# Adding up the squares of a normalisation on GpSimd, with one matmul with ones behind the first weight chunk

## The chip, the cores and the metric

The kernel runs on one core of one Trainium2 chip. The metric is the device time of the whole kernel in microseconds (us), here the median of 3 runs.

## The reference

A first block and a two-layer second block work on 256 tokens of width 1024 (the first one with 16 meta tokens ahead: 272). There are six normalisations in the change's sense, in this order: before the first block's mixer (norm 0), before its FFN (norm 1), the final one of the first block together with the one before the second block's even mixer (norm 2, two sums), before the first MLP (norm 3), before the odd mixer (norm 4) and before the last MLP (norm 5). Each of them is

```python
ms = jnp.mean(xf * xf, axis=-1, keepdims=True)
y  = xf * lax.rsqrt(ms + EPS) * g
```

and what follows is a matrix product of y with a weight matrix. The FFN is `(silu(u @ w_gate) * (u @ w_up)) @ w_down`, an MLP is `square(relu(h @ w1)) @ w2`.

## The kernel before

**Layout.** Everything is kept with the features on the 128 partitions and the tokens along the free dimension: `x_all` is 8 feature blocks of 272 tokens. The mean over the features is therefore a sum over partitions and over 8 blocks, and it is made on TensorE: a matmul of a 128x128 matrix of ones with the squares of one block, accumulated over 8 blocks, leaves the sum on every partition. The root of it is taken late: the projections work on `u = x * gain`, and what comes out of them is multiplied by `rms` (1/root) when it is read out of PSUM.

**Split matmuls.** Weights and activations are held as a high and a low part (`whi`, `wlo` and `u[:, 0]`, `u[:, 1]`), and a product is three matmuls. ScalarE makes the high part of a weight chunk (L967), VectorE the low part (L1317, recorded at L1304), and the same holds for `u`: ScalarE `u_hi`, VectorE the low half (`lo_pair`, L1348, recorded at L1307), pair of blocks by pair, which raises `u_ready`.

**Weight chunks.** SyncE streams chunks of at most 128x2048 through a ring of 4. A chunk of 256 output columns is two groups of 8 x 3 = 48 matmuls in all, into two of four PSUM banks (`proj`), by turns; `proj_free` says that VectorE has read them out.

**The normalisation.** ScalarE, in `norm` (L1083), makes for each of four pairs the two `u_hi` and the squares of the pair (`sq_ready`), in norm 2 also the squares for the second sum; then it waits for `sumsq`, takes the square root (`root`, L975, with a table load ahead of it) and raises `root_ready`. VectorE's `norm_scale` (L1598) makes the reciprocal and raises `rms_ready`. In norm 2 a second root and reciprocal follow (L1670 to L1677).

**The ones matmuls.** TensorE's first chunk behind a normalisation has a gate, `by_pair` (L404): ahead of blocks 0, 2, 4 and 6 of its first half it waits for `u_ready` of that pair. From norm 1 on the gate also issues the ones matmuls of the pair before it (`square_pair`, L437), and at block 6 those of the last pair as well:

```python
if k % 2 == 0:
    if norm_no and k:
        square_pair(k // 2 - 1, norm_no, **sums)
    if norm_no and k == 6:
        square_pair(3, norm_no, **sums)
    pe.wait_ge(sems["u_ready"], 4 * norm_no + k // 2 + 1)
```

So `sumsq` is raised in the middle of the chunk's first half. In norm 0 all eight stand behind the first chunk (L474). The first chunk is rq0 (norm 0), the first up chunk of the FFN (norm 1), sq0 (norm 2), the first up chunk of the first MLP (norm 3), the gates chunk with 8 columns (norm 4) and the first up chunk of the last MLP (norm 5).

**The hidden layers** (`hidden_layer`, L698 on TensorE, L1602 on VectorE): TensorE does up chunk 0, up chunk 1, then the down chunk of hidden block 0 into `aux`, and from then on up and down by turns in a loop. The down chunk waits for `hidden_ready`. VectorE's order ahead of it is: reciprocal of the norm, the low part of one more weight chunk, then the first hidden block (with ScalarE's tanh in the FFN and ScalarE's high part in both), then its low half.

**GpSimd** has two instructions in the whole kernel (L1291, L1293), for the first block's attention. Each instruction of VectorE, ScalarE and GpSimd here is followed by a wait for its own semaphore (`Lane.post`).

## Time and profile before

| | |
|---|---|
| median of 3 runs | 1213.16 us (1211.6 to 1213.25) |
| the profiled execution: its span | 1212.2 us |
| TensorE matmul busy | 1131.0 us, 93%, 8618 records |
| TensorE weight loads busy | 1072.7 us, 88% |
| VectorE busy | 786.8 us, 65%, 865 records |
| ScalarE busy | 514.3 us, 42%, 509 records |
| GpSimd busy | 6.0 us, 6 records |
| DMA | 175.70 MB, 145 GB/s in the mean |

The profile gives no time of its own for the profiled execution beside the span; the median of the timed runs is 0.9 us above the span. The span counts from the start of the first record to the end of the last. Busy time of TensorE is modelled (matmuls overlap with the next one), so the starts of matmuls are what is read for a rate. One matmul of 32-bit floats with `ones` leaves two records, one split matmul leaves one. DVE is VectorE, ACT is ScalarE, POOL is GpSimd, PE is TensorE. In brackets at a row's end stands how long the engine had been idle before it and who ended that.

### The profile page before, as it was taken

What the parts mean: (1) busy time and instruction counts of PE and PEld (TensorE: products, weight loads), DVE (VectorE), ACT (ScalarE), POOL (GpSimd) and SP (SyncE); (2) the same over time, 40 slices, a digit from 0 to 9 for tenths busy, and PEclk for the clock granted to TensorE, in tenths of its full rate; (3) what the DMA queues carried; (4) which work ended last, traced back from release to release, by engine and by line L of the source; (5) the groups of instructions that cost most, each with busy time, mean ns of one, the idle gap of its engine ahead of it and who ended that gap; (6) DMA issues with size and microseconds to landing.
All of it is one profiled execution on the core that took longest, in us unless ns stands there. A gap on an engine that the chain in (4) does not pass through costs nothing.

```text
span 1212.2 us, 20954 instructions
## 1 busy us (share of the span) xinstructions
PE 1131.0 (93%) x8618; PEld 1072.7 (88%) x8618; DVE 786.8 (65%) x865; ACT 514.3 (42%) x509; POOL 6.0 (0%) x6
## 2 busy tenths in 40 slices
PE   5998999799899999988986999999988999999998
PEld 4996777588899999988875999999988899999997
DVE  4765778577656665667677565555469787655553
ACT  5323443333444444446274543433244356434331
POOL 0000001000000000000000000000000000000000
PEclk9998999799999999999997999999988999999999
DMA  8743135034435656563421365564343434655630
GB/s 259 228 139 105 40 106 172 8 124 134 140 90 170 192 173 205 166 215 127 161 95 44 131 209 171 176 207 132 113 139 105 143 114 162 208 184 167 202 104 35
DMA packets 160534, 175.70 MB, mean 145 GB/s; under 512 B 4433, under 2 KB 146769, under 8 KB 160353
## 3 DMA queue, kind: packets, MB, share of 16 engines
q1 hardware_dynamic: 160480, 174.95, 45.7%
q8 instruction: 39, 0.64, 0.2%
q14 instruction: 15, 0.11, 0.0%
HBM read 173.89 MB, written 1.05 MB: 144 GB/s over the span
## 4 chain that ended last, share of the span: by engine, by line
PE 77%; DVE 15%; ACT 5%; issue 2%; DMA 0%; SPq 0%; DVEq 0%; ACTq 0%
PE proj L384 47%; PE aux L725 20%; DVE f L1307 4%; DVE wlo L1304 4%; DVE f L1304 2%; PE aux L441 2%; DVE f L1310 1%; ACT whi L967 1%; PE aux L652 1%; PE aux L528 1%; PE aux L635 1%; DVE x_all L1304 1%; DVE v L1307 1%; PE aux L522 1%; PE aux L645 0%
## 5 line engine op out<-in xcount | busy, mean ns | idle before, releaser
L384 PE MATMUL proj<-u,whi 128*128 128x256 f32 (+1 forms) x2912 | 540.7, 287 | 18.9 <-DVE wlo L1304 8.9
L384 PEld LDWEIGHTS proj<-u,whi 128*128 128x128 f32 x2912 | 457.5, 192 | 28.9 <-issue 19.9
L1304 DVE TENSOR_TENSOR wlo<-raw,whi 128x2048 fp32r<-128x2048 f32 (+2 forms) x175 | 374.1, 2137 | 145.0 <-ACT whi L967 138.4
L384 PE MATMUL proj<-u,wlo 128*128 128x256 f32 (+1 forms) x1456 | 414.5, 285 | 0.0
L967 ACT ACTIVATE whi<-raw 128x2048 fp32r<-128x2048 f32 (+2 forms) x175 | 313.5, 1791 | 131.3 <-PE proj L384 78.1
L384 PEld LDWEIGHTS proj<-u,wlo 128*128 128x128 f32 x1456 | 279.8, 192 | 0.0
L725 PE MATMUL aux<-v,whi 128*128 128x256 f32 x1376 | 249.9, 283 | 1.7 <-DVE v L1304 1.5
L725 PEld LDWEIGHTS aux<-v,whi 128*128 128x128 f32 x1376 | 214.2, 192 | 2.4 <-issue 2.4
L725 PE MATMUL aux<-v,wlo 128*128 128x256 f32 x688 | 194.6, 283 | 0.0
L725 PEld LDWEIGHTS aux<-v,wlo 128*128 128x128 f32 x688 | 131.9, 192 | 0.0
L384 PE MATMUL proj<-v,whi 128*128 128x256 f32 (+2 forms) x592 | 112.5, 292 | 9.2 <-DVE v L1304 3.7
L384 PEld LDWEIGHTS proj<-v,whi 128*128 128x128 f32 (+1 forms) x592 | 94.0, 194 | 13.3 <-issue 10.8
L1138 ACT ACTIVATE v<-f 128x512 fp32r<-128x512 f32 x32 | 20.2, 632 | 166.8 <-DVE f L1304 166.8
L384 PE MATMUL proj<-v,wlo 128*128 128x256 f32 (+2 forms) x296 | 84.9, 287 | 0.0
L384 PE MATMUL proj<-whi,u 128*128 128x256 f32 (+1 forms) x352 | 68.1, 289 | 5.5 <-DVE f L1310 2.5
L384 PEld LDWEIGHTS proj<-whi,u 128*128 128x128 f32 x352 | 57.6, 197 | 7.3 <-issue 5.6
L1304 DVE TENSOR_TENSOR v<-f,v 128x512 fp32r<-128x512 f32 (+2 forms) x56 | 34.0, 607 | 38.5 <-ACT v L1138 24.7
L384 PEld LDWEIGHTS proj<-v,wlo 128*128 128x128 f32 (+1 forms) x296 | 57.3, 193 | 0.0
L1304 DVE TENSOR_TENSOR f<-proj,r_all 128x512 f32<-128x512 f32 (+6 forms) x67 | 40.9, 610 | 22.2 <-PE proj L384 19.7
L1310 DVE TENSOR_SCALAR f<-proj 128x512 f32<-128x512 f32 x32 | 22.1, 692 | 44.6 <-PE proj L384 44.0
L384 PE MATMUL proj<-wlo,u 128*128 128x256 f32 (+1 forms) x176 | 50.2, 285 | 0.0
L1131 ACT ACTIVATE proj<-f 128x256 f32<-128x256 f32 x22 | 8.5, 388 | 66.0 <-DVE f L1304 66.0
(248 smaller groups left out, 842.4 us busy)
## 6 DMA issues: line engine op xcount, KB each, us to landing
raw<-in_mlp_w_dram SPq DMA_DIRECT2D x64, 1024.0 KB, 5.4
raw<-in_w_in_dram SPq DMA_DIRECT2D x22, 1024.0 KB, 5.3
raw<-in_od_w_in_dram SPq DMA_DIRECT2D x12, 1024.0 KB, 5.5
raw<-in_w_ffn_gate_dram SPq DMA_DIRECT2D x22, 512.0 KB, 4.0
raw<-in_w_ffn_up_dram SPq DMA_DIRECT2D x22, 512.0 KB, 5.3
raw<-in_w_ffn_down_dram SPq DMA_DIRECT2D x21, 512.0 KB, 5.5
raw<-in_ev_w_in_dram SPq DMA_DIRECT2D x10, 1024.0 KB, 5.9
raw<-in_w_ret_out_dram SPq DMA_DIRECT2D x4, 1024.0 KB, 5.4
```

The lines of the kernel that those rows point to most:

```text
L384: ins = mm(o, w_of(a, k), x_of(b, k), start=first and k == 0 and j == 0, stop=last and k == kt - 1 and j == 2, skip_group_check=skip)
L441: ins = mm(aux[:, 0, 0:tokens], C("ones"), sq_of(tokens)[:, k, :], start=k == 0, stop=k == KT - 1, skip_group_check=True)
L522: ins = mm(o, k_ret[p0:p0 + 64, h // 2, t:t + m], q_ret[p0:p0 + 64, h // 2, :], start=True, stop=True)
L528: ins = mm(aux[:, 2 * (h % 2) + 1, S:2 * S], rv_tok[0:m, j, h * P:(h + 1) * P], sd[0:m, h % 2, j, :], start=j == 0, stop=j == 2)
L635: ins = mm(aux[:, b, 0:L], q_all[0:96, h, b * P:(b + 1) * P], k_all[0:96, h, :], start=True, stop=True)
L652: ins = mm(aux[p0:p0 + 64, 3, S:2 * S], v_tok[0:m, j, 64 * h:64 * h + 64], pt[0:m, j, :], start=j == 0, stop=j == 2)
L725: ins = mm(aux[:, j // 2, (j % 2) * S:(j % 2 + 1) * S], W(a, n, 0, kt, D)[:, q, j * P:(j + 1) * P], v[:, b, 2 * (k % 2) + q, :], start=fir ...
L967: A.post(act(whi[:, n % RING, 0:wd], raw[:, n % RING, 0:wd], ACT.Copy), "hi_ready")
L1138: A.post(act(v[:, 0, 2 * (k % 2):2 * (k % 2) + 2, :], f("f1", 512, 2, S), ACT.Copy), "hidden_hi")
L1304: return ve.tensor_tensor(o, a, b, op)
L1307: return ve.scalar_tensor_tensor(out=o, in0=a, scalar=s, in1=b, op0=op0, op1=op1)
L1310: return ve.tensor_scalar(o, a, s, s2, op) if op2 is None else ve.tensor_scalar(o, a, s, s2, op, op2)
```

## The change

The squares are no longer summed over the blocks on TensorE. GpSimd gets a function `add_squares`: when the squares of pair c are ready it adds that pair to pair 0 (an operation of 128x512, in place; in norm 2 one for each sum), and after pair 3 it adds block 1 to block 0 (128x256) and raises `sq_added` (and `second_added`). TensorE's gate only waits for `u_ready`. Behind the whole first chunk `sum_squares` waits for `sq_added` and issues one ones matmul, in norm 2 two. Nothing else is changed. In norm 0 the operations are 128x544 and 128x272 wide.

```diff
--- before.py
+++ after.py
@@ -401,14 +401,10 @@
             def finish(ins):
                 ins.then_inc(sems["chunk_used"], 1)
 
-            def by_pair(norm_no, **sums):
+            def by_pair(norm_no):
 
                 def gate(k):
                     if k % 2 == 0:
-                        if norm_no and k:
-                            square_pair(k // 2 - 1, norm_no, **sums)
-                        if norm_no and k == 6:
-                            square_pair(3, norm_no, **sums)
                         pe.wait_ge(sems["u_ready"], 4 * norm_no + k // 2 + 1)
                 return gate
 
@@ -434,19 +430,14 @@
                                    lambda a, k: W(a, n, 0, KT, width)[:, k, :], KT, gate=gate if j == 0 else None)
                 finish(ins)
 
-            def square_pair(c, norm_no, tokens=S, second=False):
-
-                pe.wait_ge(sems["sq_ready"], 4 * norm_no + c + 1)
-                for k in (2 * c, 2 * c + 1):
-                    ins = mm(aux[:, 0, 0:tokens], C("ones"), sq_of(tokens)[:, k, :], start=k == 0, stop=k == KT - 1,
-                             skip_group_check=True)
-                if second and c:
-
-                    for k in range(0 if c == 1 else 2 * c, 2 * c + 2):
-                        ins = mm(aux[:, 1, 0:S], C("ones"), f("f3", 0, KT, S)[:, k, :], start=k == 0, stop=k == KT - 1,
-                                 skip_group_check=True)
-                if c == 3:
-                    ins.then_inc(sems["sumsq"], 1)
+            def sum_squares(norm_no, tokens=S, second=False):
+
+                pe.wait_ge(sems["sq_added"], norm_no + 1)
+                ins = mm(aux[:, 0, 0:tokens], C("ones"), sq_of(tokens)[:, 0, :], start=True, stop=True)
+                if second:
+                    pe.wait_ge(sems["second_added"], 1)
+                    ins = mm(aux[:, 1, 0:S], C("ones"), f("f3", 0, KT, S)[:, 0, :], start=True, stop=True)
+                ins.then_inc(sems["sumsq"], 1)
 
             def turn_norm(norm_no):
 
@@ -471,8 +462,7 @@
             project("rq0", t0=META, t=S, gate=by_pair(0))
             pe.wait_ge(sems["const_in"], 16)
             pe.wait_ge(sems["x_ready"], KT)
-            for c in range(4):
-                square_pair(c, 0, L)
+            sum_squares(0, L)
             project("rq1", t0=META, t=S)
             project("rk0")
             read_out("rq1")
@@ -733,6 +723,7 @@
 
                 pe.wait_ge(sems["proj_free"], order[g - 1] if order[g - 1] % 2 else order[g - 1] + 1)
                 up(g, 0, gate=by_pair(norm_no))
+                sum_squares(norm_no)
                 pe.wait_ge(sems["proj_free"], order[g - 1] + 1)
                 up(g + 1, 1)
                 pe.wait_ge(sems["rms_ready"], norm_no + 1)
@@ -748,7 +739,8 @@
 
 
             pe.wait_ge(sems["hidden_val"], M0["k0"])
-            project("sq0", t0=META, t=S, gate=by_pair(2, second=True))
+            project("sq0", t0=META, t=S, gate=by_pair(2))
+            sum_squares(2, second=True)
             for name in ("sq1", "sk0", "sk1"):
                 project(name, t0=META, t=S)
             turn_norm(2)
@@ -854,6 +846,7 @@
 
             pe.wait_ge(sems["hidden_val"], M1["k0"])
             project_tokens("gates", 8, gate=by_pair(4))
+            sum_squares(4)
             project("qk0", t0=META, t=S, between=lambda: turn_norm(4))
 
             pe.wait_ge(sems["gates_ready"], 1)
@@ -1286,11 +1279,26 @@
             G = Lane(eng, sems, "pool_step")
             gp = nc.gpsimd
 
+            def add_squares(norm_no, tokens=S, second=False):
+
+                pairs = [(sq if tokens == L else f("f2", 0, KT, S), "sq_added")]
+                if second:
+                    pairs.append((f("f3", 0, KT, S), "second_added"))
+                for c in range(1, 4):
+                    eng.wait_ge(sems["sq_ready"], 4 * norm_no + c + 1)
+                    for t, _ in pairs:
+                        G.run(gp.tensor_tensor(t[:, 0:2], t[:, 0:2], t[:, 2 * c:2 * c + 2], ALU.add))
+                for t, name in pairs:
+                    G.post(gp.tensor_tensor(t[:, 0], t[:, 0], t[:, 1], ALU.add), name)
+
+            add_squares(0, L)
             eng.wait_ge(sems["kr_roped"], 1)
             eng.wait_ge(sems["kv_half"], 1)
             G.post(gp.tensor_copy(k_all[64:96, :, :], bc(kr[64:96, :], 8)), "kr_copied")
             eng.wait_ge(sems["q_mla_rotated"], 2)
             G.post(gp.tensor_tensor(q_pre[0:96], q_pre[0:96], bc(C("cos_mla")[0:96, META:L], 8), ALU.mult), "q_cos")
+            for norm_no in range(1, 6):
+                add_squares(norm_no, second=norm_no == 2)
 
 
         @block.vector
```

TensorE's queue at the first up chunk of the FFN (norm 1) before, from the chunk's sixth split matmul on; L384 is a split matmul, L441 a ones matmul:

```order
L441 MATMUL aux<-f,cst 128x256 x2
L384 MATMUL proj<-u,whi 128x256 x2
L384 MATMUL proj<-u,wlo 128x256
L384 MATMUL proj<-u,whi 128x256 x2
L384 MATMUL proj<-u,wlo 128x256
L441 MATMUL aux<-f,cst 128x256 x2
L384 MATMUL proj<-u,whi 128x256 x2
L384 MATMUL proj<-u,wlo 128x256
L384 MATMUL proj<-u,whi 128x256 x2
L384 MATMUL proj<-u,wlo 128x256
L441 MATMUL aux<-f,cst 128x256 x4
```

and after the change, from the end of that chunk (L436 is the ones matmul, in front of it stand the 48 of the chunk):

```order
L384 MATMUL proj<-u,whi 128x256 x2
L384 MATMUL proj<-u,wlo 128x256
L436 MATMUL aux<-f,cst 128x256
L384 MATMUL proj<-u,whi 128x256 x2
L384 MATMUL proj<-u,wlo 128x256
L384 MATMUL proj<-u,whi 128x256 x2
```

The ones matmul that raises `sumsq` has moved from behind the chunk's 18th split matmul to behind its 48th, and the eight have become one.

GpSimd's queue before (the first three rows are the program's start):

```order
L2036 MEMSET const-bfloat16-1.0 128x1
L2036 MEMSET const-uint8-127 128x1
L1284 UNCONDITIONAL_BRANCH
L1291 COPY f<-kr 32x2176
L1293 ISA
L1293 TENSOR_TENSOR f<-f,cst 96x2048
```

and after the change, from norm 0 to norm 2:

```order
L1290 TENSOR_TENSOR f<-f 128x544 x3
L1292 TENSOR_TENSOR f<-f 128x272
L1297 COPY f<-kr 32x2176
L1299 TENSOR_TENSOR f<-f,cst 96x2048
L1290 TENSOR_TENSOR f<-f 128x512 x3
L1292 TENSOR_TENSOR f<-f 128x256
L1290 TENSOR_TENSOR f<-f 128x512 x6
L1292 TENSOR_TENSOR f<-f 128x256 x2
```

The two old instructions stand behind the adds of norm 0; each of the norms 3 to 5 adds three rows of 128x512 and one of 128x256 more.

## Rows read from the trace of the kernel before

**Rows 1.** Busy times by stretch (PE, PEld, DVE, ACT, POOL, PEclk, DMA): last MLP

```profile
1042.00:1190.00 148.00, 148.00 (x1244) 148.00 (x1244) 86.99 (x66) 56.27 (x39) 0.00 (x0) 1.00 0.49 163
```

**Rows 2.** The ones matmuls' line: min/median/max ns, first and last start

```profile
L441 PE MATMUL aux<-f,cst x96: 377/379/774, 27.8 to 1022.5; 128*128 128x256 f32 x80, 128*128 128x272 f32 x16
```

**Rows 3.** Timeline of GpSimd: start us, us, engine, line, operation, tiles, form

```profile
210.37 3.82 POOL L1293 TENSOR_TENSOR f<-f,cst 96x2048 f32<-96x2048 f32 x1 [1.03 <-PE aux L606]
```

**Rows 4.** Timeline at norm 1 (FFN), TensorE, VectorE and ScalarE, by start

```profile
343.63 0.50 PE L384 MATMUL proj<-u,whi 128*128 128x256 f32 x2 [0.85 <-DVE x_all L1304]
...
344.28 1.03 DVE L1307 SCALAR_TENSOR_TENSOR u<-x_all,par,u 128x256 fp32r<-128x256 f32 x2 [0.70 <-ACT u L1094]
...
344.75 0.63 ACT L1095 ACTIVATE f<-x_all 128x512 f32<-128x512 f32 x1
...
347.56 1.89 PE L441 MATMUL aux<-f,cst 128*128 128x256 f32 x8
...
349.53 1.28 ACT L976 ACT_TABLE_LOAD   x1 [4.15 <-PE aux L441]
...
353.35 2.29 DVE L1304 TENSOR_TENSOR wlo<-raw,whi 128x2048 fp32r<-128x2048 f32 x1 [0.19 <-ACT whi L967]
...
359.46 0.42 DVE L1304 TENSOR_TENSOR v<-f,v 128x256 fp32r<-128x256 f32 x1 [0.61 <-ACT v L1134]
...
360.04 0.47 PE L725 MATMUL aux<-v,whi 128*128 128x256 f32 x2 [1.37 <-DVE v L1304]
```

**Rows 5.** Timeline at norm 2 (two sums), by start

```profile
548.80 1.03 DVE L1307 SCALAR_TENSOR_TENSOR u<-x_all,small,u 128x256 fp32r<-128x256 f32 x2 [1.70 <-ACT u L1094]
...
549.93 1.05 ACT L1100 ACTIVATE f<-x_all,par 128x256 f32<-128x256 f32 x2
...
553.02 2.29 DVE L1304 TENSOR_TENSOR wlo<-raw,whi 128x2048 fp32r<-128x2048 f32 x1 [3.20 <-ACT whi L967]
...
553.81 1.28 ACT L976 ACT_TABLE_LOAD   x1 [0.89 <-PE aux L446]
...
566.65 0.50 PE L384 MATMUL proj<-u,whi 128*128 128x256 f32 x2 [3.73 <-DVE wlo L1304]
```

**Rows 6.** Timeline at norm 3 (first MLP)

```profile
691.34 1.28 ACT L976 ACT_TABLE_LOAD   x1 [4.16 <-PE aux L441]
```

**Rows 7.** Timeline at norm 4 (gates)

```profile
878.32 2.05 DVE L1307 SCALAR_TENSOR_TENSOR u<-x_all,par,u 128x256 fp32r<-128x256 f32 x4
...
885.29 0.47 ACT L976 ACTIVATE r_all<-aux,small 128x256 f32<-128x256 f32 x1 [3.25 <-PE aux L441]
...
887.81 4.62 DVE L1304 TENSOR_TENSOR wlo<-raw,whi 128x2048 fp32r<-128x2048 f32 x2 [0.19 <-ACT whi L967]
...
898.22 0.60 PE L862 MATMUL aux<-cst,small 128*4 128x128 f32 x4 [1.76 <-DVE small L1307]
```

**Rows 8.** Timeline at norm 5 (last MLP)

```profile
1017.14 0.40 PE L384 MATMUL proj<-u,whi 128*128 128x256 f32 x2
...
1019.33 1.03 DVE L1307 SCALAR_TENSOR_TENSOR u<-x_all,par,u 128x256 fp32r<-128x256 f32 x2 [0.70 <-ACT u L1094]
...
1022.96 1.28 ACT L976 ACT_TABLE_LOAD   x1 [2.53 <-PE aux L441]
```

**Rows 9.** Busy times by stretch (PEclk is the granted clock), norms 2 and 4

```profile
567.40:570.80 3.40, 3.40 (x18) 3.40 (x18) 3.37 (x2) 0.00 (x0) 0.00 (x0) 0.50 0.92 293
...
875.00:885.00 10.00, 10.00 (x33) 8.65 (x33) 7.35 (x11) 5.61 (x8) 0.00 (x0) 0.51 0.00 0
```

**Rows 10.** Timeline at norm 0, VectorE and TensorE

```profile
26.42 6.95 DVE L1304 TENSOR_TENSOR wlo<-raw,whi 128x2048 fp32r<-128x2048 f32 x3
...
33.62 1.85 DVE L1370 RECIPROCAL r_all<-r_all 128x272 f32<-128x272 f32 x1 [0.25 <-ACT r_all L976]
...
35.51 0.69 DVE L1304 TENSOR_TENSOR f<-proj,r_all 128x512 f32<-128x512 f32 x1
...
37.16 0.42 PE L384 MATMUL proj<-u,whi 128*128 128x272 f32 x2
```

## The prediction

> **What bounds the kernel now.** I read the page first: TensorE is busy for 93% of the span, so a change that takes matmuls away looks like a gain of their length. I then read the timeline of every place where the removed matmuls stand, because an average says nothing about what a place is worth. There are six: the normalisations 0 to 5, each in the first weight chunk behind it.
>
> In the long hidden loops TensorE is the bound: 148.0 of 148.0 us busy with 1,244 matmuls at the full clock [rows 1], so one split matmul of 256 columns takes 0.119 us, and a chunk of 48 takes 5.7 us. A ones matmul has two records: [rows 2] counts 96 at L441, which are 48 matmuls, and 8 more stand in the second sum of norm 2. The group of four in [rows 4] takes 1.89 us with the tail of its last one, so one costs about 0.43 us. The change keeps 7 of 56, and 49 x 0.43 = **21.1 us** of TensorE's work go. That is the number one would like to forecast, and I don't.
>
> The reader is to see in [rows 4] what waits for these matmuls. In the FFN the last four start at 347.56, ScalarE begins the table load for the root at 349.53, VectorE makes the reciprocal, splits a weight chunk (353.35, 2.29 us), then comes the first hidden block, and its low half is written from 359.46 for 0.42 us. TensorE meanwhile does the rest of chunk one and all of chunk two, is out of work, and starts the down projection at 360.04 **after waiting 1.37 us for that low half**. The chain from the root's start to the down projection is 360.04 - 349.53 = 10.5 us, and nothing in the change shortens it. What counts in this place is therefore when the sum leaves TensorE, not how much TensorE works.
>
> **The change, place by place.** The last ones matmul moves from the middle of the first chunk to behind it. From the start of the last one to the root's start is 349.53 - (347.56 + 3 x 0.43) = 0.7 us, and stays so.
>
> *Norm 1 (FFN).* TensorE starts the chunk at 343.63; u is complete when VectorE's two operations from 344.28 end, 345.31, before the fourth pair is due (343.63 + 18 x 0.119 = 345.8). So the chunk runs through: 343.63 + 5.7 = 349.3, one ones matmul from there to 349.8, the root at 350.0. That is **0.5 us later than 349.53**, although seven matmuls fewer were done. GpSimd has to be ready by 349.3: the last squares end at 344.75 + 0.63 = 345.4, then one add of 512 and one of 256. The nearest row is its product of 96x2048 in 3.82 us [rows 3]: by its elements 0.95 and 0.48 us, at worst 3.82 each. I take the first, since the row is the same operation, and GpSimd is ready at 347. The chain then puts the down projection at 360.04 + 0.5. TensorE ends chunk two at 349.8 + 5.7 = 355.5 and now waits 5.0 us where it waited 1.4. Net: **+0.5 us**.
>
> *Norm 3 (first MLP).* The same shape, with the root's start at 691.34 [rows 6]. The down projection starts there without a listed wait, so its chain and chunk two end together; now the one comes 0.5 us later and the other 3 us earlier: some 3.5 us of waiting. **+0.5 us**.
>
> *Norm 5 (last MLP).* Here u is complete late: 1019.33 + 1.03 = 1020.4, when TensorE, started at 1017.14, has long done its 18 matmuls. It waits, then does 30 more (3.6 us) to 1024.0, root at 1024.7 against 1022.96 [rows 8]. **+1.7 us**, and again some 4 us of waiting before the down projection.
>
> *Norm 2 (two sums).* Sixteen ones matmuls fill the time between pairs of u; the root starts at 553.81 [rows 5]. Without them TensorE waits for each pair: ScalarE has five operations per pair and VectorE ends the last low half at 548.80 + 1.03 = 549.8. The last squares end at 549.93 + 1.05 = 551.0. GpSimd then has two adds of 512 and two of 256, 2.9 us by the low price: 553.9. TensorE's last 30 matmuls end at 553.4 at the full clock and, if part of them runs at half clock, at 555 to 556. With two ones matmuls the root starts between 555.0 and 558. I take 557, **+3.2 us**. Behind it stands a chain of root, two reciprocals, a second root and the first lo split of chunk sk0, for which TensorE already waits 3.73 us (566.65), so all of it counts.
>
> *Norm 4 (gates).* The chunk's columns are 8 wide and TensorE stood at half clock there: 0.51 from 875 to 885 [rows 9]. Now it waits for u_ready until 880.4, then issues 30 of these at 0.21 us (half clock): 886.7, and the root at 887.9 with the ones matmul at half clock, against 885.29. VectorE's two splits behind the reciprocal end at 887.81 + 4.62 = 892.4 now, about 1 us before TensorE's turned factors come; they will end 2.6 us later, so the transposes at 898.22 start about **1.7 us** later [rows 7]. At the full clock the same sum gives -1.6 us, the other end.
>
> *Norm 0.* Seven of eight ones matmuls go, 3.0 us, and chunk rq1 starts earlier, though not before its lo half, the first of three splits from 26.42 on, at 28.7. Chunk rk0 needs rq0's bank, and VectorE frees it only behind all three splits (33.37), a reciprocal of 1.85 us and 0.69 us for the bank [rows 10]: 36.0 where TensorE started at 37.16. **-1.1 us**.
>
> The sum is 0.5 + 0.5 + 1.7 + 3.2 + 1.7 - 1.1 = **+6.5 us**.
>
> **What the new waits do to the clock.** The granted clock was 0.50 from 567.4 to 570.8, right behind the wait of 3.73 us that ended at 566.65, and 18 matmuls ran there where 0.119 us each would have made 28 [rows 5, 9]. The new waits before the down projections of norms 1, 3 and 5 are 5.0, 3.5 and about 4 us, and behind each TensorE is the bound. I take one such stretch and a little more each, 1.9 us; the ends are nothing and 3.4 us. **+5.7 us**. The Trainium skill (TensorE: Matmul & The Clock Gate, Part 1) says that the default state is the slow one and that activity releases it; that rule speaks against a change that takes filler work off TensorE where it waits, and by it the sum is +12.2, without it +6.5.
>
> Together **+12.2 us**. Sum and rows are of one execution with a span of 1212.2 us; the median of the timed runs is 0.9 us above that span, and I add the difference to the median: 1213.2 + 12.2 = 1225.4 us.
>
> **The rivals.** (a) *The clock stays up* at the three down projections: 1213.2 + 6.5, about **1220 us**; with norms 2 and 4 at their low ends (+1.2 and -1.6) it is +1.2 in all, 1214. For it: the wait of 1.37 us in [rows 4] is short, and the waits of 3.5 and 4 us may be shorter than I make them. Against it: the one wait as long as these in the rows was followed by it.
>
> (b) *GpSimd and VectorE get in each other's way, or an add costs far more than 0.95 us.* The adds of norm 2 would meet the split at 553.02 (2.29 us), and those of norm 5 the low halves of u; one operation of VectorE in front of the last add and one add in front of u's low half cost 2.3 + 1.0 us in norm 2 and 1.0 in norm 5. That is 4 us more, about **1230 us**. With adds of 3.8 us norms 1, 3 and 5 have 7.6 us of adds where 3.9 us are free (345.4 to 349.3), 3.7 us more each, **1238 us** or beyond. No row here shows the two engines reading SBUF at once with two SBUF inputs on VectorE's side. The Trainium skill (SBUF — State Buffer, section SBUF: two separate sides) has the port pair that the two share as an exclusive lock, held for a whole instruction, for a VectorE operation with two SBUF inputs; no run here shows that so far.
>
> (c) *The other side, faster:* TensorE's busy time is what bounds, and the chain from the sum to the first hidden block fits behind chunk two. The point from which it decides is a chain of no more than the 5.7 us of that chunk. Then each removed matmul counts: 1213.2 - 21.1 = **1192 us**. For it: the 93%. Against it: the chain measures 10.5 us, and TensorE waits for it already, with 3 us more of cover. For a small gain it would be enough that norms 2 and 4 gain instead of losing.
>
> (d) *No change:* the later roots cost less than worked out (the chain has slack that [rows 4] doesn't show, at norms 3 and 5), and the -1.1 of norm 0 and a gain in norm 4 balance the rest: **1213 us**.
>
> **How the numbers follow.** Forecast, chains and clock: 0.52. (a) 0.20, (b) 0.15, (d) 0.08, (c) 0.05. The range has to hold 8 in 10. Its low end takes in (a), 1216, its high end the 1230 of (b) and clock stretches of twice the length, 1233; the 1238 of (b), (c) and (d) stay outside. A measurement of this kernel can tell about 0.2%, 2.4 us, from no change. Slower by over that: forecast, (b), nearly all of (a), 0.86; within it: (d) and the low end of (a), 0.09; faster: 0.05.
>
> **What would show it.** In the changed profile TensorE's busy time should fall by less than 21 us as modelled ends stretch at half clock, its waits in the first chunks of norms 2, 4 and 5, and before the down projection's first matmul, should rise from 1.4 to about 5 us (FFN) and from nothing to some 3.5 to 4 us (both MLPs), with the table load of the root 0.5 us later counted from the chunk's start. The clock should be at half behind them. The release of the root by GpSimd instead of by the chunk's end would show (b); no wait before the down projections would show the forecast wrong, and a span under 1200 us would mean that I misread what bounds these places.

## The result, and the profile after

The changed kernel takes **1237.4 us** (median of 5 runs, 1234.55 to 1239.85), the kernel before, timed beside it, 1213.05. The ratio is 1.0207, interval 1.0194 to 1.022: **24.3 us slower**, where the forecast had 12.2. The direction was right, and the time lies outside the range of 1216 to 1233.

Part 1 of the page after, TensorE's busy time first:

```profile
span 1235.4 us, 20803 instructions
## 1 busy us (share of the span) xinstructions
PE 1126.9 (91%) x8520; PEld 1070.9 (87%) x8520; DVE 800.2 (65%) x865; ACT 514.2 (42%) x509; POOL 43.9 (4%) x34
```

98 matmul records are gone (49 matmuls of two records each), and TensorE's busy time fell by 4.1 us, not by 21: matmuls that run at the half clock are counted longer. I added up the stretches in which the granted clock is at its lower level, 1.2 GHz: 81.1 us before, 138.1 after. The rise is largest in the even mixer (17.1 to 37.5 us), in norm 2 up to its root (4.7 to 15.5) and in the odd mixer (13.7 to 21.0).

The two traces can be cut at the same instructions: the first matmul of the chunk behind each norm, the activation of its root (1.3 us behind the table load's start), and the first down matmul. What each step takes more than before:

| step | forecast | measured |
|---|---|---|
| norm 0 and the first mixer | -1.1 | -3.94 (see the last experiment) |
| norm 1: chunk to root; root to down | +0.5; 0 | +0.53; 0.00 |
| FFN's loop behind its first down | +1.9 | +2.48 |
| norm 2: chunk to root | +3.2 | **+5.36** |
| even mixer: that root to norm 3's chunk | 0 | **+4.97** |
| norm 3: chunk to root; root to down | +0.5; 0 | +0.55; 0.00 |
| first MLP's loop | +1.9 | +1.44 |
| norm 4: chunk to root | part of the next | **+4.36** |
| odd mixer, up to norm 5's chunk | +1.7 with norm 4 | -0.19 |
| norm 5: chunk to root; root to down | +1.7; 0 | **+5.09**; 0.00 |
| last MLP's loop | +1.9 | +2.51 |
| sum | +12.2 | +23.2 |

The sum is that of two single executions, 1.1 us under the difference of the medians.

**The FFN and the MLPs went as forecast.** Timeline after at norm 1, TensorE, ScalarE and GpSimd; it answers to [rows 4]:

```profile
341.58 1.29 POOL L1290 TENSOR_TENSOR f<-f 128x512 f32<-128x512 f32 x1 [3.71 <-ACT f L1088]
342.95 0.73 POOL L1292 TENSOR_TENSOR f<-f 128x256 f32<-128x256 f32 x1
346.12 1.28 ACT L969 ACT_TABLE_LOAD   x1 [4.67 <-PE aux L436]
356.62 0.77 PE L715 MATMUL aux<-v,whi 128*128 128x256 f32 x2 [4.95 <-DVE v L1312]
...
710.51 0.77 PE L715 MATMUL aux<-v,whi 128*128 128x256 f32 x2 [3.67 <-DVE v L1312]
...
1052.84 0.77 PE L715 MATMUL aux<-v,whi 128*128 128x256 f32 x2 [3.64 <-DVE v L1312]
```

GpSimd is done at 343.7, long before the chunk's end. The waits are 4.95, 3.67 and 3.64 us where 5.0, 3.5 and about 4 were worked out. The clock behind them (windows: PE busy and count, PEld, DVE, ACT, POOL, PEclk, DMA share, GB/s; the second window is in the last MLP):

```profile
355.40:362.20 6.80, 5.58 (x26) 5.61 (x27) 3.38 (x7) 3.29 (x5) 0.00 (x0) 0.50 0.60 162
1052.80:1058.50 5.70, 5.66 (x26) 5.69 (x27) 3.68 (x3) 1.80 (x2) 0.00 (x0) 0.50 0.48 144
1057.00:1185.00 128.00, 128.00 (x1071) 128.00 (x1070) 74.86 (x58) 50.98 (x35) 0.00 (x0) 0.99 0.57 189
```

In 5.7 us 26 matmuls run where 48 would at the full clock. Afterwards the loop runs as in [rows 1], and what it lost is never won back.

**Norm 2 did not.** VectorE, GpSimd, ScalarE and TensorE after, answering to [rows 5]:

```profile
544.53 8.71 POOL L1290 TENSOR_TENSOR f<-f 128x512 f32<-128x512 f32 x6 [200.85 <-ACT f L1093]
545.15 5.61 DVE L1315 SCALAR_TENSOR_TENSOR u<-x_all,small,u 128x256 fp32r<-128x256 f32 x4
550.81 0.79 PE L384 MATMUL proj<-u,whi 128*128 128x256 f32 x2 [1.18 <-DVE u L1315]
552.09 3.31 DVE L1312 TENSOR_TENSOR wlo<-raw,whi 128x2048 fp32r<-128x2048 f32 x1 [1.33 <-ACT whi L960]
553.33 3.47 POOL L1292 TENSOR_TENSOR f<-f 128x256 f32<-128x256 f32 x2
557.56 0.59 PE L439 MATMUL aux<-f,cst 128*128 128x256 f32 x2
558.23 1.28 ACT L969 ACT_TABLE_LOAD   x1 [6.25 <-PE aux L439]
571.06 0.79 PE L384 MATMUL proj<-u,whi 128*128 128x256 f32 x2 [7.24 <-DVE wlo L1312]
```

The split at 552.09 takes 3.31 us, not the 2.29 of [rows 5]. The arithmetic of these rows is that of whole instructions taking turns. The six adds end at 544.53 + 8.71 = 553.24. The split waits for that, 1.15 us at most, and is 1.02 us longer. GpSimd's next add starts at 553.33, the split ends at 555.40: 2.07 us of waiting and two adds of 0.73 make 3.5, and the row has 3.47. GpSimd ends at 553.33 + 3.47 = 556.80. TensorE starts the 30 matmuls behind the last pair at 550.81 and the first ones matmul at 557.13, so they took 6.3 us where 3.6 would do at the full clock; the granted clock was at half there until 556.8. The two chains end within 0.4 us of each other, and both are late: making only one of them faster gains little. In the kernel with fillers below, TensorE is done first and waits for GpSimd, and norm 2 is still 4.78 us longer than before:

```profile
554.34 0.70 PE L443 MATMUL aux<-f,cst 128*128 128x256 f32 x2 [1.47 <-POOL f L1300]
```

Behind the root the wait for sk0's low half grew from 3.73 to 7.24 us, and the clock is at half behind that, too:

```profile
567.40:577.60 10.20, 6.54 (x31) 6.54 (x32) 9.88 (x10) 2.89 (x3) 0.00 (x0) 0.52 0.55 182
604.60:611.40 6.80, 6.80 (x28) 5.87 (x27) 4.37 (x3) 0.00 (x0) 0.00 (x0) 0.50 0.12 43
```

The second window lies 45 us behind the root. TensorE is full there in both kernels; the window at the same distance in the trace of before has 59 matmuls:

```profile
600.20:607.00 6.80, 6.80 (x59) 6.63 (x61) 4.44 (x4) 0.00 (x0) 0.00 (x0) 1.00 0.29 88
```

Followed matmul by matmul, the even mixer loses 1.2 us directly behind the wait, 3.1 us in the stretch 45 us behind the root and some 0.6 us in waits near its end. The long wait is no sufficient reason for the second stretch. With the adds alone (first experiment) the wait is longer still and the stretch is missing; in the hybrid (below) the wait is that of before and the stretch is there. Each pair is the matmul behind the wait and the window 44 to 52 us behind the root, adds alone first:

```profile
568.59 0.80 PE L384 MATMUL proj<-u,whi 128*128 128x256 f32 x2 [8.52 <-DVE wlo L1324]
602.00:608.80 6.80, 6.80 (x55) 6.27 (x53) 4.17 (x3) 0.00 (x0) 0.00 (x0) 1.00 0.24 74
```

```profile
560.12 0.51 PE L384 MATMUL proj<-u,whi 128*128 128x256 f32 x2 [3.68 <-DVE wlo L1320]
592.30:599.10 6.80, 6.80 (x27) 5.83 (x26) 4.46 (x3) 0.00 (x0) 0.00 (x0) 0.50 0.13 45
```

**Norm 4**, after, VectorE, GpSimd and TensorE, answering to [rows 7]:

```profile
886.93 1.37 POOL L1290 TENSOR_TENSOR f<-f 128x512 f32<-128x512 f32 x1 [188.11 <-ACT f L1088]
887.22 1.89 DVE L1315 SCALAR_TENSOR_TENSOR u<-x_all,par,u 128x256 fp32r<-128x256 f32 x2
889.13 1.27 POOL L1290 TENSOR_TENSOR f<-f 128x512 f32<-128x512 f32 x1 [0.82 <-ACT f L1088]
889.14 0.69 DVE L1315 SCALAR_TENSOR_TENSOR f<-aux,r_all 128x512 f32<-128x512 f32 x1
889.87 1.08 DVE L1312 TENSOR_TENSOR x_all<-x_all,f 128x512 f32<-128x512 f32 x1
892.04 0.37 PE L384 MATMUL proj<-whi,u 128*128 128x8 f32 x1 [1.44 <-DVE u L1315]
899.74 1.20 PE L436 MATMUL aux<-f,cst 128*128 128x256 f32 x2
912.87 1.01 PE L855 MATMUL aux<-cst,small 128*4 128x128 f32 x4 [3.71 <-DVE small L1315]
```

While GpSimd adds (889.13 to 890.40), an operation that reads PSUM (`aux`) takes its usual 0.69 us, and the one behind it, with both inputs in SBUF, 1.08 instead of 0.69. From the last wait to the ones matmul TensorE issues 36 narrow matmuls in 7.7 us. I had counted 30 from the fourth pair on; at half clock TensorE was still busy with the third pair when the fourth came. The transposes behind the turned factors wait 3.71 us where [rows 7] had 1.76, and lie 3.3 us later, counted from the chunk's start, where 1.7 was forecast. The root is 4.36 us later there, so 1.1 us is won back between the root and the transposes.

**Norm 5**, after, answering to [rows 8]:

```profile
1027.94 1.53 POOL L1290 TENSOR_TENSOR f<-f 128x512 f32<-128x512 f32 x1 [132.98 <-ACT f L1088]
1028.35 1.93 DVE L1315 SCALAR_TENSOR_TENSOR u<-x_all,par,u 128x256 fp32r<-128x256 f32 x2
1032.96 1.51 POOL L1290 TENSOR_TENSOR f<-f 128x512 f32<-128x512 f32 x1 [3.48 <-ACT f L1088]
1033.36 1.91 DVE L1315 SCALAR_TENSOR_TENSOR u<-x_all,par,u 128x256 fp32r<-128x256 f32 x2
1037.77 0.56 PE L384 MATMUL proj<-u,whi 128*128 128x256 f32 x2 [1.48 <-DVE u L1315]
```

Two of u's low halves are longer by 0.9 us each, and both stand on the way to the last pair. TensorE then runs at half clock inside the chunk; the 30 matmuls from 1037.77 to the ones matmul at 1042.94 take 5.2 us where 3.6 would do:

```profile
1038.10:1041.50 3.40, 3.40 (x18) 3.40 (x17) 0.00 (x0) 0.00 (x0) 1.83 (x2) 0.50 0.00 0
```

### The profile page after: what moved, and what is told of

It reads as the page before. It is cut to its first block, busy times and chain, and to the rows that moved or that the text cites. A ratio compares the mean times of both kernels' runs of the same rounds, so it can differ in the third digit from the quotient of the medians.

```text
span 1235.4 us, 20803 instructions
## 1 busy us (share of the span) xinstructions
PE 1126.9 (91%) x8520; PEld 1070.9 (87%) x8520; DVE 800.2 (65%) x865; ACT 514.2 (42%) x509; POOL 43.9 (4%) x34
## 4 chain that ended last, share of the span: by engine, by line
PE 71%; DVE 19%; ACT 7%; issue 3%; DMA 0%; SPq 0%; DVEq 0%; ACTq 0%
PE proj L384 44%; PE aux L715 20%; DVE wlo L1312 5%; DVE f L1315 4%; DVE f L1312 3%; DVE u L1315 2%; ACT whi L960 2%; DVE f L1318 1%; PE aux L642 1%; DVE x_all L1312 1%; PE aux L625 1%; DVE v L1315 1%; PE aux L635 0%; DMA f<-in_x_dram 0%; PE aux L518 0%
## 5 line engine op out<-in xcount | busy, mean ns | idle before, releaser
L384 PE MATMUL proj<-u,whi 128*128 128x256 f32 (+1 forms) x2912 | 547.1, 289 | 33.0 <-DVE u L1315 12.6
L384 PEld LDWEIGHTS proj<-u,whi 128*128 128x128 f32 x2912 | 463.0, 194 | 44.3 <-issue 21.7
L384 PE MATMUL proj<-u,wlo 128*128 128x256 f32 (+1 forms) x1456 | 417.6, 287 | 0.0
L384 PEld LDWEIGHTS proj<-u,wlo 128*128 128x128 f32 x1456 | 283.4, 195 | 0.0
L715 PE MATMUL aux<-v,whi 128*128 128x256 f32 x1376 | 255.9, 287 | 12.4 <-DVE v L1312 12.4
L715 PEld LDWEIGHTS aux<-v,whi 128*128 128x128 f32 x1376 | 219.3, 196 | 13.1 <-issue 13.1
L715 PEld LDWEIGHTS aux<-v,wlo 128*128 128x128 f32 x688 | 134.9, 196 | 0.0
L384 PE MATMUL proj<-v,whi 128*128 128x256 f32 (+2 forms) x592 | 112.6, 292 | 9.2 <-DVE v L1312 3.7
L384 PEld LDWEIGHTS proj<-v,whi 128*128 128x128 f32 (+1 forms) x592 | 94.0, 194 | 13.3 <-issue 10.8
L384 PE MATMUL proj<-v,wlo 128*128 128x256 f32 (+2 forms) x296 | 85.1, 287 | 0.0
L384 PE MATMUL proj<-whi,u 128*128 128x256 f32 (+1 forms) x352 | 72.3, 300 | 11.0 <-DVE u L1315 5.9
L384 PEld LDWEIGHTS proj<-whi,u 128*128 128x128 f32 x352 | 61.9, 212 | 13.0 <-issue 6.0
L1290 POOL TENSOR_TENSOR f<-f 128x512 f32<-128x512 f32 (+1 forms) x21 | 30.8, 1465 | 816.3 <-ACT f L1088 596.6
L384 PEld LDWEIGHTS proj<-v,wlo 128*128 128x128 f32 (+1 forms) x296 | 57.4, 194 | 0.0
L384 PE MATMUL proj<-wlo,u 128*128 128x256 f32 (+1 forms) x176 | 52.4, 298 | 0.0
```

What stands on the lines that cost most here:

```text
L384: ins = mm(o, w_of(a, k), x_of(b, k), start=first and k == 0 and j == 0, stop=last and k == kt - 1 and j == 2, skip_group_check=skip)
L715: ins = mm(aux[:, j // 2, (j % 2) * S:(j % 2 + 1) * S], W(a, n, 0, kt, D)[:, q, j * P:(j + 1) * P], v[:, b, 2 * (k % 2) + q, :], start=fir ...
L1290: G.run(gp.tensor_tensor(t[:, 0:2], t[:, 0:2], t[:, 2 * c:2 * c + 2], ALU.add))
```

## The experiments

Three theories. **A**: GpSimd's adds hold up VectorE, by rival (b)'s lock. **B**: the sum comes later, because it stands behind 48 matmuls and not inside the chunk. **C**: what is lost is the clock, since matmuls that filled TensorE's waits are gone. Each ratio is against the kernel before, run beside it; where two of the kernels are compared, it is by their medians. The kernel before had medians between 1212.2 and 1213.3 beside the different experiments, so such a comparison can be off by about 1 us.

**Adds alone.** The kernel before, with GpSimd's adds into an unused tile, and ScalarE waiting for them ahead of the root:

```diff
+                eng.wait_ge(sems["sq_added"], norm_no + 1)
                 eng.wait_ge(sems["sumsq"], norm_no + 1)
...
+            for norm_no in range(1, 6):
+                add_squares(norm_no, second=norm_no == 2)
```

> The kernel before, its 56 ones matmuls all in place, with GpSimd's adds made as in the change but into a scratch region that only the root waits for (the result isn't used). Theory A (GpSimd's adds and VectorE's operations with two SBUF inputs hold each other up): the low halves of u stretch as in the changed kernel, 5.4 us for four in norm 0 and 5.6 us for four in norm 2, and of the 24 us some 5 to 8 are here, 1218 to 1221 us, from norms 2, 4 and 5. Theory B (only the later sum costs) and theory C (only the clock, by the missing matmuls): GpSimd works beside and the time is that of before, 1213 within 1.5 us.

Measured: 1223.44, ratio 1.0086 (1.0069 to 1.0103), **+10.4** by the ratio. Norm 2's root is 4.44 later, norm 5's 1.58, norm 4's 0.66; norms 1 and 3 0.04. There, too, low halves of u meet an add and take 0.9 us longer (1.92 us for two, 1.01 before), but VectorE would have waited for TensorE behind them. Adds whose result nobody uses cost 6.7 us in the norms, within the 5 to 8 expected. A holds. The total is above the 1218 to 1221 of the expectation: the even mixer takes 1.59 and the odd one 2.62 us more, and the first one 2.5 us less in this one trace. The kernel of memsets below has such losses in the mixers without an add, so they can't be put down to A.

**Move alone.** No GpSimd; all 8 (16) ones matmuls behind the chunk.

```diff
                 up(g, 0, gate=by_pair(norm_no))
+                for c in range(4):
+                    square_pair(c, norm_no)
```

> The kernel before without GpSimd, with its eight (in norm 2 sixteen) ones matmuls all behind the first chunk. Theory B: the root starts later by about 3.4 us in norms 1 and 3 than before (chunk 5.7 us and then eight matmuls of 0.43 us), 3.5 or more in norm 5, 3 to 6 in norm 2 and 2 to 3 in norm 4, and all of it counts: 1228 to 1232 us. If only GpSimd matters (theory A alone), TensorE does the same work in another order and the time stays within 2 us of before. Theory C adds that the clock falls in the gaps between the pairs of norm 2 although no matmul was taken away, since they moved.

Measured: 1249.86, 1.0299 (1.0281 to 1.0318), **+37**. Behind the chunk the ones matmuls stand on the way to the root. Timeline at norm 1:

```profile
348.82 3.62 PE L437 MATMUL aux<-f,cst 128*128 128x256 f32 x16
...
363.01 0.77 PE L721 MATMUL aux<-v,whi 128*128 128x256 f32 x2 [4.91 <-DVE v L1306]
```

Norms 1 and 3 lose 3.55 us each, as expected, norm 2 8.9, norm 4 7.5 and norm 5 4.8. Behind the longer waits the three loops lose 5.6 us and the even mixer 4.5. B as a mechanism holds; its size was taken far too low in norms 2 and 4, and what the clock adds in loops and mixer was left out. Most of this the change avoids by having one matmul there: its norm 1 loses 0.53.

**Fillers.** The changed kernel, with ones matmuls on constants where TensorE waits:

```diff
                 pe.wait_ge(sems["rms_ready"], norm_no + 1)
+                filler(10 if tag == "ffn" else 7)
                 down(g + 2, 0, first=True)
...
+                        if norm_no == 2:
+                            filler({2: 1, 4: 3, 6: 1}.get(k, 0))
                         pe.wait_ge(sems["u_ready"], 4 * norm_no + k // 2 + 1)
```

> The changed kernel with ones matmuls of constants (results unused) where TensorE waits: one, three and one in norm 2 between the pairs, and in front of the first down projection ten in the FFN and seven in each MLP, issued behind rms_ready. They add 29 matmuls, 12.5 us, of TensorE's work, all of it within waits. Theory C: the half-clock stretches behind the waits of norms 1, 3 and 5 (6.8, 3.4 and 6.8 us long in the changed kernel) go and those of norm 2 and of the even mixer get shorter: 5 to 10 us less than the changed kernel, 1227 to 1232. Theories A and B alone: the same as the changed kernel, 1237 within 2 us, or more by what doesn't fit into the waits.

Measured: 1225.66, 1.012 (1.0099 to 1.0141), so 11.7 us of the loss come back. Timeline, norm 1:

```profile
352.25 4.48 PE L407 MATMUL aux<-cst 128*128 128x256 f32 x20
357.36 0.48 PE L722 MATMUL aux<-v,whi 128*128 128x256 f32 x2 [0.63 <-DVE v L1320]
```

and the clock there:

```profile
350.00:360.00 10.00, 9.37 (x63) 8.53 (x62) 6.12 (x8) 3.84 (x6) 0.00 (x0) 1.00 0.38 105
```

The steps of the three loops become 0.00, from +2.48, +1.44 and +2.51. The down projection starts no earlier by its own chain; it runs at the full clock, and that alone is worth 6.4 us. Most of the rest of the 11.7 lies in the even mixer (+4.97 to +2.01), which has 20.5 us at half and not 37.5, and in norm 5 (+5.09 to +3.59), whose chunk runs at the full clock here; norm 2 gets only 0.6 us better. The time is a little under the 1227 to 1232 expected. For the three loops this is C, shown. The Trainium skill (TensorE: Matmul & The Clock Gate, Part 1) has activity release the slow state; the filled and the unfilled wait agree with it.

**Sum inside the chunk.** `sum_squares` stands behind 36 split matmuls of 48, through a gate on the chunk's second half:

```diff
+                def gate(k):
+                    if k == 4:
+                        sum_squares(norm_no, **kw)
```

> The changed kernel with its ones matmul inside the chunk, behind 36 of its 48 split matmuls (12 earlier), in norms 1 to 5. Theory B: the root and with it the down projection starts 1.4 us earlier in norms 1, 3 and 5 and about 2 us earlier in norm 4; in norm 2 hardly, since GpSimd's second sum is ready only at the chunk's end there: 5 to 7 us less than the changed kernel, 1231 us. If the later sum doesn't matter (theories A or C alone): no difference beyond 2 us.

Measured: 1228.65, 1.0131 (1.0114 to 1.0148). Norms 1 and 3 are at -0.90 against before, 1.4 better than behind the chunk; norm 2 is unchanged at +5.32, and norm 5 at +3.70. The later place costs what the sum said in norms 1 and 3, and does not explain norm 2. In all it gains 8.7 us against the changed kernel, more than the 5 to 7 expected; norm 4 (+4.36 to +1.80) and the FFN's loop (+2.48 to +1.50) are part of that.

**Adds on VectorE.** The changed kernel; the adds leave GpSimd's queue and stand behind `lo_pair` in VectorE's.

```diff
                     lo_pair(c, gain, norm_no)
+                    add_pair(c, norm_no)
```

> The changed kernel with its adds on VectorE instead of GpSimd (same order, same places of the ones matmuls). Theory A: what GpSimd's adds cost beside VectorE (10.6 us alone in e1) goes, VectorE's own adds (0.7 and 0.4 us each) put back 1 to 3 us on the path in norm 2, where six and two stand behind the last low half: 1228 to 1231 us. If GpSimd's adds cost only through what they trigger in the clock, or theories B and C hold alone: 1235 us or more.

Measured: 1229.37, 1.0145 (1.0127 to 1.0162): **8.0 us faster than on GpSimd** (7.2 if each is first taken against its own runs of the kernel before), although VectorE now does 5.25 us of adds in norm 2 itself:

```profile
545.92 1.03 DVE L1300 SCALAR_TENSOR_TENSOR u<-x_all,small,u 128x256 fp32r<-128x256 f32 x2 [1.71 <-ACT u L1087]
546.99 5.25 DVE L1297 TENSOR_TENSOR f<-f 128x512 f32<-128x512 f32 x8
```

Norm 2 goes from +5.36 to +2.51, the even mixer from +4.97 to +1.17, norm 4 from +4.36 to +3.10.

**Memsets in place of the adds.** The kernel of adds alone, with `gp.memset` for `gp.tensor_tensor`: the same queue, waits and semaphores.

```diff
-                        G.run(gp.tensor_tensor(o, t[:, 0:2] if c == 1 else o, t[:, 2 * c:2 * c + 2], ALU.add))
+                        G.run(gp.memset(o, 1.0))
```

> As e1, but with memsets of the same size on GpSimd in place of the adds, behind the same waits: GpSimd writes and reads nothing. Theory A as a matter of reading: VectorE's operations with two SBUF inputs keep their length (2.1 us for four in norms 0 and 2) and the time is that of before, 1213 within 2 us. If any use of SBUF by GpSimd holds VectorE up, or what cost 10.6 us in e1 is the waits and semaphores of GpSimd: 1217 us or more.

Measured: 1218.6, 1.0051 (1.0037 to 1.0066). By the total this misses the 1213 of the expectation and lies where it had put semaphores or any use of SBUF, 1217 or more; the steps say otherwise. Norm 0's low halves, with adds first (adds alone) and memsets second:

```profile
19.23 5.35 POOL L1302 TENSOR_TENSOR f<-f 128x544 f32<-128x544 f32 x3 [18.78 <-ACT f L990]
20.37 5.41 DVE L1327 SCALAR_TENSOR_TENSOR u<-x_all,par,u 128x272 fp32r<-128x272 f32 x4
```

```profile
19.64 1.24 POOL L1302 MEMSET f<- 128x544 f32 x2 [0.20 <-ACT f L990]
20.05 2.11 DVE L1327 SCALAR_TENSOR_TENSOR u<-x_all,par,u 128x272 fp32r<-128x272 f32 x4
```

5.41 us against 2.11, and the steps of norms 1 to 5 are within 0.22 us of before. So it is not GpSimd's semaphores or its writing, but an add, which reads SBUF. The memsets are also shorter (0.55 us against some 1.3), but two of them do overlap the low halves, and leave no mark. A GpSimd instruction that reads SBUF without adding was not tried. The Trainium skill (SBUF — State Buffer, section SBUF: two separate sides) says that a port pair shared by the two engines is held for a whole instruction by whichever starts first, when VectorE has two SBUF inputs and GpSimd reads. Rows and rule agree: the turns of norm 2, and the untouched PSUM operation of norm 4. What stays at +5.5 us lies in the mixers (even +1.65, odd +3.90), at half clock in other places than before. The 3.90 arise within 15 us of norm 4's root, where this kernel is at half clock without a break (877.3 to 897.8 us, 11.4 us of it behind the root) and the kernel before is at half for 3.4 us of the same stretch. Why is open.

**Norms 2 and 4 undone.** The changed kernel, with the old gates and no adds there.

```diff
-            for norm_no in range(1, 6):
-                add_squares(norm_no, second=norm_no == 2)
+            for norm_no in (1, 3, 5):
+                add_squares(norm_no)
```

> The changed kernel with norms 2 and 4 as before (their 24 ones matmuls on TensorE in the gate, no adds on GpSimd there). From the difference of the two traces the steps from the start of the chunk to the root cost 5.4 us in norm 2 and 4.4 in norm 4, and the even mixer behind norm 2 cost 5.0 us. If the even mixer's loss hangs on norm 2 (by the longer wait in front of sk0 and the clock): 1237 - 14.8 = 1222 to 1224 us. If it comes from elsewhere: 1227 to 1228.

Measured: 1225.31, 1.0108 (1.0094 to 1.0123). This lies between the two forecasts, nearer the first. The even mixer falls from +4.97 to +0.65: its loss hangs on norm 2, though this doesn't say by which of the things changed there. Norm 5, where two low halves are still 0.9 us longer, keeps +3.59, which is the forecast's 1.7 and the lock's 1.8; its chunk is at the full clock here.

**Both cures.** The changed kernel with the edits of both experiments, VectorE's adds and the fillers (1, 3, 1 in norm 2's gates, 10 and 7 before the down projections).

> The changed kernel with both cures at once: its adds on VectorE (alone: 1229.4 against 1237.4) and the filler matmuls in norm 2's gates and before the down projections (alone: 1225.7). The fillers' product is overwritten. If the two losses are separate and add up, 1237.4 - 8.0 - 11.8 = 1217.6; by the steps: loops nothing (they were +1.97, +2.62, +2.50 with the adds on VectorE), norm 2 some +1.5, norm 4 +3.1, norm 5 +4.7, norm 0 -1 = 1221. Above 1224 the two overlap, and one of them was counted twice.

Measured: 1224.05, 1.0093 (1.0068 to 1.0118). The two cures took 8.0 and 11.7 us off, and together 13.4: they overlap by 5 to 6. The losses are not independent: both cures act on the even mixer (+4.97 to +1.17 and to +2.01, together +1.28) and on norm 2. Left are norm 2 (+2.13), norm 4 (+3.09) and norm 5 (+4.75), where the adds now stand in VectorE's way; norm 5's chunk has 3.4 us at half besides.

**A hybrid.** Old gates in norms 2 and 4. In the others the adds on VectorE, one ones matmul inside the chunk (behind 24 split matmuls in norms 1 and 3, behind 30 in norm 5) and a few fillers.

```diff
-                        if norm_no and k:
+                        if norm_no in (2, 4) and k:
                             square_pair(k // 2 - 1, norm_no, **sums)
...
+                    if k == (2 if norm_no == 5 else 0):
+                        sum_squares(norm_no)
...
+                filler({1: 3, 3: 0, 5: 2}[norm_no])
                 down(g + 2, 0, first=True)
```

> The kernel before in norms 2 and 4. In norms 0, 1, 3 and 5 VectorE adds the squares and one ones matmul follows, in norm 0 behind the chunk, in norms 1 and 3 behind 24 of its 48 split matmuls, in norm 5 behind 30. Three and two ones matmuls of constants stand in the waits before the down projections of norms 1 and 5 (not used in the result). All theories together: the root starts 2.2 us earlier than before in norms 1 and 3, 0.4 us in norm 5, norm 0 gives 1.0 us, no lock and no missing filler: 5 to 6 us faster than before, 1207 us. If the clock falls all the same behind the waits of 1 to 2 us: 1210 to 1213.

Measured: 1210.28, 0.9984 (0.9974 to 0.9994). Norms 1 and 3 gain 2.06 each; norm 5 loses 1.07; the even mixer takes 3.59 back. The time falls into the forecast's second branch (1210 to 1213), but not for its reason: the clock doesn't fall behind the waits before the down projections (loops 0.01, -0.01 and +0.34).

**Norms 0, 1 and 3 only.** As the hybrid, with norm 5 as before:

```diff
+                    if k == 0 and norm_no != 5:
+                        sum_squares(norm_no)
...
+                filler({1: 3, 3: 0, 5: 0}[norm_no])
                 down(g + 2, 0, first=True)
```

> The part of the change that the traces bear out, alone: the kernel before, with norms 2, 4 and 5 untouched, and in norms 0, 1 and 3 the adds on VectorE and one ones matmul (norms 1 and 3 in front of the second 24 split matmuls of the chunk, three filler matmuls in front of the FFN's down projection, whose product is overwritten). The steps of norms 1 and 3 should be -2.1 us each as in the hybrid, norm 0 about -1.0, norms 2, 4 and 5 and the loops nothing: 1213.1 - 5.2 = 1208. If the half-clock stretches in the mixers are simply placed anew by every shift of what is ahead of them (as the even mixer of the hybrid, +3.6, and the odd mixer of the memset kernel, +3.9, say), the total can be anywhere from 1206 to 1212, and the difference will stand in the mixers and not in the norms.

Measured: 1209.53 against 1213.28, **0.9968 (0.9958 to 0.9977): faster than both kernels**, by 3.8 us. Timeline, norm 1:

```profile
344.60 0.70 PE L454 MATMUL aux<-f,cst 128*128 128x256 f32 x2
353.64 1.46 PE L458 MATMUL aux<-cst 128*128 128x256 f32 x6
355.89 0.47 PE L740 MATMUL aux<-v,whi 128*128 128x256 f32 x2 [0.80 <-DVE v L1320]
```

The ones matmul that raises `sumsq` starts 3.1 us behind the chunk's start instead of 5.2. Here the removed matmuls are worth something, because the one that is left stands early enough; the wait behind is filled. Norms 1 and 3 give the 2.06 us each again. In the profiled execution, the slowest of the ten, the even mixer takes 2.16 and the odd one 2.83 us back, which is the second half of the expectation.

**Norms 1 and 3 only.** As the last one, with norm 0's eight ones matmuls back:

```diff
-            sum_squares(0, L)
+            for c in range(4):
+                square_pair(c, 0, L)
```

> As the kernel of norms 0, 1 and 3, with norm 0 also as before: so two places of six changed. Norms 1 and 3 -2.1 us each, everything else nothing: 1213.1 - 4.1 = 1209. The first mixer has nothing changed ahead of it and must be the same to 0.1 us; the even mixer lies 2.1 us earlier in the span and the odd one 4.1 us, with no instruction in them or ahead of them in their norms changed: if their length still moves by a microsecond or more, it is the placing of the half-clock stretches against the work that does it, and not anything in the norms.

Measured: 1210.76, 0.9982 (0.9973 to 0.9991). Norms 1 and 3 -2.06 each, as expected (the time, 1210.76, is above the 1209 summed up); the first mixer -0.15; norm 2's root -0.62; but the even mixer +2.20. A piece of it 46 us behind the root, full of matmuls, now has a half-clock stretch:

```profile
598.00:601.40 3.40, 3.40 (x18) 3.40 (x17) 3.06 (x2) 0.00 (x0) 0.00 (x0) 0.51 0.00 0
```

**The kernel before, a second profile,** with no edit.

> The kernel before, unedited, profiled a second time. Open is whether a half-clock stretch that an experiment has and the profile of before has not (in the even mixer, +2.2 in the kernels of norms 1 and 3 and of norms 0, 1 and 3; in the odd mixer, +3.9 in the memset kernel) belongs to the kernel or to the one execution. If to the kernel, the mixers here are 130.3 and 131.9 us as in the first profile, to 0.3 us, and the half-clock stretches in them are the same. If to the execution, one or more of the mixers differs by 1 us or more, and losses of the mixers count only as a mean over runs. The normalisations and the hidden loops should be the same to 0.1 us either way.

Measured: span 1210.0 where the first had 1212.2. Norm 1's chunk starts 2.56 us earlier than in the first profile, all of it from the first mixer (-3.0); the even and the odd mixer are the same to 0.1 us, as are their half-clock stretches and the loops. Nearly all of the 3.0 arises where the first profile is at half from 106.6 to 116.9 us and the second does that work at the full clock. So the first mixer's length belongs to the execution, and the -3.94 of the table is no gain of the change: against this second profile it is -1.4, near the forecast's -1.1. The differences in the even and odd mixers stood still in this one repetition and look like the kernel's; one repetition is thin evidence for it.

## Why the prediction was right and wrong

The forecast's +12.2 is 11.0 short of the +23.2 of the traces. By terms: even mixer 5.0, norm 5 3.4, norm 4 with the odd mixer 2.5, norm 2 2.2, the clock behind the three waits 0.7, norms 1 and 3 0.1, and norm 0 with the first mixer 2.8 the other way, of which 2.6 belong to the execution.

- **TensorE's 21 us are not to be had**: right. Its busy time fell by 4.1 us and the kernel got slower.
- **Norms 1 and 3, +0.5 each**: right (+0.53, +0.55). **The clock behind the three new waits, 5.7**: right in mechanism and near in size, 6.4, and shown by the fillers, which took it to nothing.
- **Norm 0, -1.1**: rk0 starts at 36.16 where it started at 37.16, -1.0. GpSimd stretches the low halves there from 2.11 to 5.41 us, but into idle time.
- **Norm 2, +3.2**: the first step that failed. "GpSimd then has two adds of 512 and two of 256, 2.9 us by the low price" was short twice. The adds cost 1.27 and 0.73 us, not 0.95 and 0.48. And with VectorE they take turns: GpSimd ended 6.8 us behind the last squares (550.05), and the last low half of u came 1.9 us later than before, counted from the chunk's start. TensorE's 30 matmuls behind it, most of them at half clock, ended at the same time as GpSimd. It measured 5.36; with the adds on VectorE 2.51.
- **The even mixer, nothing**: the step that is missing. I carried norm 2's loss to the root and stopped. It measured +4.97, the largest miss. Behind the root the wait of 3.73 us became 7.24, and the clock there costs 1.2 us. I had shown in [rows 9] that a stretch follows the wait at 566.65, and applied it only to the *new* waits, not to the one that my own sum made longer. The larger part, 3.1 us, is the half-clock stretch 45 us behind the root. That the loss hangs on norm 2 is shown (+0.65 with norm 2 undone); why the clock falls 45 us later is not, and the length of the wait doesn't settle it.
- **Norm 4, +1.7**: the root had been put 2.6 us later (887.9 against 885.29) and is 4.36 later. 1.3 of the 1.8 over that is the lock, since with the adds on VectorE it is +3.10; the rest is in the main the third pair, which TensorE at half clock had not finished when the fourth came. The cover I saw behind the root (from 2.6 down to 1.7) was there as far as the transposes, which won back 1.1; the odd mixer as a whole gave back 0.19, with 21.0 us at half clock where it had 13.7. The low end that I gave for norm 4, -1.6 at the full clock, doesn't come out of its own terms either: 880.4, 30 matmuls at half the price (3.1) and 0.7 to the root make 884.2 against 885.29, so about -1.
- **Norm 5, +1.7**: +5.09. 1.7 as worked out, 1.8 of the lock, and 1.6 of half clock inside the chunk (30 matmuls in 5.2 us, where 3.6 would do at 0.119 us each). Without that half clock it is 3.59, in the kernels of the fillers and of norms 2 and 4 undone.
- **The rivals**: (b), the lock, was true, and its 4 us on top gave 1230 with a chance of 0.15. The rival's weight was wrong: its condition, a VectorE operation with two SBUF inputs while GpSimd adds, could be read off the order of both queues; operations meet in all six norms and cost time in norms 2, 4 and 5. Its price was also held to VectorE's own delay, without the clock that a longer wait costs. (a), (c) and (d) are out.

Open, besides the stretch behind norm 2: why a kernel that is the same up to a shift of 2 to 3 us, and 0.6 us in a norm, gets a half-clock stretch in a full piece of the even mixer (+2.2) that the kernel before lacks in both of its profiles. No run tried to place such a stretch on purpose.

## What to carry to other kernels

In this kernel the work that TensorE did while it would have waited anyway was free twice: it cost nothing, and it held the clock up behind the wait. Before such matmuls are removed, look for what TensorE waits on next; where the chain from the sum is what bounds, gain comes only from making the sum leave earlier, as in the version of norms 0, 1 and 3. An add moved to GpSimd is not free either: hold its place against every VectorE operation with two SBUF inputs, and count both the waiting and what it does to the next wait.

## What was not expected of the hardware

- One add of 128x512 on GpSimd takes 1.27 to 1.29 us undisturbed, one of 128x256 0.73 us; VectorE's low half of u beside them takes 0.9 us longer, its split of 128x2048 1.02 us longer.
- Half-clock stretches also turn up where TensorE has work throughout: 28 matmuls in 6.8 us against 59, 45 us behind a root.
- Two executions of one kernel differ by 3.0 us in the first mixer, by where the half clock falls (106.6 to 116.9 us in the one, 100.9 to 104.3 in the other).
